# Feature-major FFN chunks from chunk 2 on, with another order of the blocks and other engines for the small additions

## The chip, the cores and the metric

The kernel runs on one core of a Trainium2 chip. The metric is the device time of one execution in microseconds (us). The kernel before takes 999.14 us, the median of three runs (998.72 to 999.98).

## The reference, cut to what matters

Two layers act on x of 256 tokens and 1024 features, in float32. Each layer is an FFN, a mixer, and a second FFN, and each of these adds its output to a scaled x and normalizes the rows:

```
def swiglu(x, w_in, w_out):                    # w_in 1024 x 5632, w_out 2816 x 1024
    gate, up = jnp.split(x @ w_in, 2, axis=-1)
    return (jax.nn.silu(gate) * up) @ w_out
x = layer_norm(ALPHA * x + 0.5 * swiglu(x, ffn1_w_in[l], ffn1_w_out[l]), ...)
x = layer_norm(ALPHA * x + mixer(x), ...)
x = layer_norm(ALPHA * x + 0.5 * swiglu(x, ffn2_w_in[l], ffn2_w_out[l]), ...)
```

The change touches the four FFNs alone. The mixers (differential attention with pooling in the first layer, a gated linear recurrence in the second) stay as they are.

## The kernel before, in words

The phases run in the order F0, AB, F1, F2, C, F3; the F's are FFNs, AB and C the mixers. The program writes out by hand, for each engine, the order of its instructions; engines wait for each other through semaphores, and nothing is planned at run time.

Every float32 matrix is split into a rounded part (hi) and a residual (lo), and a product is taken as hi x hi + hi x lo + lo x hi. Weights come in units of 128 x 2048 numbers (1 MB, two DMAs of 512 KB) into a ring of three raw buffers. ScalarE (ACT) casts a unit to hi (`split_hi`), VectorE (DVE) subtracts to get lo (`split_lo`), and only then may SyncE's queue load the unit three further on into the same raw buffer.

An FFN goes through 11 chunks of 256 hidden features. Chunk c has two units of w_in (numbers s0+3c-1 and s0+3c from chunk 1 on) and one of w_out. Chunks 0, 1, 2 and 10 are token-major: tokens are the stationary operand, the hidden values come out by tokens, and TensorE transposes them. Chunks 3 to 9 are feature-major: weights are the stationary operand, a block of 128 hidden features by (256 tokens hi, 256 tokens lo) is made by 8 matmuls of 512 columns (L2022) and 8 of 256 columns (L2029) in one PSUM bank, G[0]. ACT copies the block out (`up_copy`, L570), its two halves are added, the gate goes through silu, and VectorE multiplies (`up_product`, L1077). The order of the four blocks is gate 0, value 0, gate 1, value 1. The halves of the first three blocks are added by an accumulating DMA from GpSimd's queue (`add_halves`, L1759), those of the fourth by VectorE (`last_up_add`, L1061). Since there is one bank, a block can start only when the block before it has been copied.

Chunks 0 to 8 of the second product aren't multiplied as they stand. They use a Strassen-like scheme of seven products in seven PSUM banks, on sums and differences of hidden blocks (`hidden_sums`) and of weight blocks (`weight_sums`): 21 matmuls (L2036) for each chunk. "Early" products (banks 0, 1, 2, 4, 5) run between the blocks of the next chunk, the "late" ones (3 and 6) one chunk later. hT_hi and hT_lo hold the split hidden operand (`hid_early_hi`, L554; `hid_late_hi`, L561).

At the end of an FFN, the tail, chunk 10 is computed token-major (`project`, L1830, L1834, L1839), and the seven banks are drained: four go through ACT or VectorE into SBUF (`kept`, `SUM_PLACES`), and VectorE adds them to x_tok with four instructions of 512 columns (L1287) and one of 1024 (L1258). Then come `down` for chunks 9 and 10 and the normalization (`norm_stats`, L1114).

The parts of the code that the change touches, with the line numbers of the profile:

Of the kernel before, what the change touches and what calls it, by code (L numbers as in the profile page):

```python
# [25 lines left out]
P = 128  # L26
# [10 lines left out]
N_COPY = 3  # L37
FIRST_FM = 3
N_FM = NC - 1 - FIRST_FM
STD_CHUNK = {0: 0, 1: 1, 2: 2, NC - 1: 3}  # L40
# [35 lines left out]
def build(nc, x, positions, ln_gain, ln_bias, ffn1_w_in, ffn1_w_out, ffn2_w_in, ffn2_w_out, ab_w_in, ab_w_o,  # L76
          diff_lambda, diff_subln, pool_w, pool_scale, c_w_in, c_w_o, c_norm, hgrn_gamma, consts, out):
    with ExitStack() as ctx:
# [68 lines left out]
        halves_added = [sem(f"halves_added{b}") for b in range(4)]  # L147
# [140 lines left out]
        def tile_half(a, t):  # L288
# [59 lines left out]
        first_halves = ffn_tok[:].rearrange("p a t f -> p (a t f)").rearrange("p (b f) -> p b f", b=2)  # L348
        HALVES = {name: [first_halves[:, 0], first_halves[:, 1], region(5376 if name == BEFORE_AB else 6656, 512),
                         region(8192 if name == BEFORE_AB else 7168, 512)] for name in FFN}  # L350
# [123 lines left out]
        def _(act):  # L474
# [88 lines left out]
            def up_copy(name, c, b):  # L563

                f = SILUS[name]
                act.wait_ge(up_done, 4 * (N_FM * f + c - FIRST_FM) + b + 1)
                if c > FIRST_FM:
                    act.wait_ge(hid_product, 2 * (N_FM * f + c - FIRST_FM - 1) + b // 2 + 1)
                dst = HALVES[name][b]
                nc.scalar.copy(dst, G[0]).then_inc(up_copied, 1)  # L570

            def up_silu(name, c, j):

                act.wait_ge(halves_added[2 * j], 16 * (N_FM * SILUS[name] + c - FIRST_FM + 1))
                gate = HALVES[name][2 * j][:, 0:SEQ]
                nc.scalar.activation(gate, gate, ACT.Silu).then_inc(gate_silu, 1)  # L576

            def ffn(name, m):
# [40 lines left out]
                n = s0 + 3 * 2 + 1  # L619
                hid_early_hi(name, 1)  # L620
                hid_late_hi(name, 1)
                if m:
                    split_hi(n + 1)
                ffn_silu(name, 0, 2, G[0])
                if m == 0:
                    split_hi(n + 1)
                split_sums_hi(name, n)
                split_hi(n + 2)
                ffn_silu(name, 1, 2, G[0])
                split_plain_hi(n + 3)  # L630
                hidT_copy(name, 2, G[0])
                last = NC - 2
                for c in range(FIRST_FM, NC - 1):
                    n = s0 + 3 * c + 1
                    split_hi(n + 1)
                    if c == FIRST_FM:
                        hid_early_hi(name, c - 1)
                    up_copy(name, c, 0)
                    split_hi(n + 2)
                    if c > FIRST_FM:  # L640
                        hid_early_hi(name, c - 1)
# [3 lines left out]
                    up_silu(name, c, 0)  # L645
# [8 lines left out]
                    up_silu(name, c, 1)  # L654
# [3 lines left out]
                nc.scalar.activation(SUM_PLACES[name][:, 0], PROD[4], ACT.Copy, scale=NORMS[name][1]  # L658
                                     ).then_inc(copied_out, 1)
                act.wait_ge(hid_product, 2 * N_FM * (f + 1))  # L660
# [314 lines left out]
        def _(dve):  # L975
# [22 lines left out]
            def weight_sums(name, n, part):  # L998
# [3 lines left out]
                t1, t2, t3, t4 = (SUM_PLACES[name][:, a] for a in range(4))  # L1002
                if part == 0:
# [3 lines left out]
                    nc.vector.tensor_tensor(t1, b12, b11, ALU.subtract).then_inc(w_step1, 1)  # L1007
                    nc.vector.tensor_tensor(t3, b22, b12, ALU.subtract)
                else:
                    dve.wait_ge(w_step1, nth[n])  # L1010
                    nc.vector.tensor_tensor(t2, b22, t1, ALU.subtract).then_inc(w_step2, 1)
# [16 lines left out]
            def hidden_sums(name, c):  # L1028
# [4 lines left out]
                if c < FIRST_FM:  # L1033
                    dve.wait_ge(hidT_copied, N_COPY * f + c + 1)
                else:
                    dve.wait_ge(hid_product, 2 * (N_FM * f + c - FIRST_FM + 1))
# [19 lines left out]
            def last_up_add(name, c):  # L1056

                f = SILUS[name]
                both = HALVES[name][3]
                dve.wait_ge(up_copied, 4 * (N_FM * f + c - FIRST_FM + 1))  # L1060
                nc.vector.tensor_tensor(both[:, 0:SEQ], both[:, 0:SEQ], both[:, SEQ:], ALU.add  # L1061
                                        ).then_inc(halves_added[3], 1)

            def up_product(name, c, j):
# [1515 lines left out]
```

## Time and profile before

| | |
|---|---|
| profiled execution | 1003.51 us |
| its span, first to last instruction | 1001.8 us |
| TensorE matmul busy | 963.8 us (96%) |
| VectorE busy | 862.0 us (86%) |
| ScalarE busy | 615.4 us (61%) |
| GpSimd busy | 109.8 us (11%) |
| mean granted TensorE clock | 0.995 |
| bytes moved | 195.72 MB, 195 GB/s |

The span is one execution, taken by the profiler. "Busy" for TensorE counts the pipelined matmuls with modelled ends, so single matmuls overlap: 8 of them in a row are shown as one stretch. "Idle before" is the time in which an engine had nothing to do, with what ended it. PE is TensorE, PEld its weight loads, DVE is VectorE, ACT ScalarE, POOL GpSimd, and SPq SyncE's DMA queue. A row of a stretch has its length, then busy time and count of PE, PEld, DVE, ACT and POOL, then the granted TensorE clock (1.00 is 2.4 GHz), the share in which the DMA engines were busy, and GB/s.

### The profile page before, as it was taken

Reading aid. Unit: us, or ns where it says so; the run is one execution under the profiler, and the core shown is the slowest. Engines: PE = TensorE matmul, PEld = TensorE weight load, DVE = VectorE, ACT = ScalarE, POOL = GpSimd, SP = SyncE. Lnnn points to the kernel's source line nnn. Section 1 sums busy time; section 2 is a strip of 40 time slices with the busy share of each in tenths; the row PEclk is TensorE's granted clock in tenths of the full one; section 3 lists DMA queues with packets and bytes.
Section 4 is the critical chain, followed back from the end, with each engine's and each line's share of the span. In section 5 each row is a group of like instructions: output and inputs, shape, how many; then the busy total and the mean of one; then the engine's idle time right before and its main releaser. Section 6 shows DMA issues by size and latency. Waiting matters only on the chain.

```text
span 1001.8 us, 13771 instructions
## 1 busy us (share of the span) xinstructions
PE 963.8 (96%) x4856; PEld 803.7 (80%) x4856; DVE 862.0 (86%) x1272; ACT 615.4 (61%) x747; POOL 109.8 (11%) x148
## 2 busy tenths in 40 slices
PE   9999999999999999999999999999999999999996
PEld 7788788788887887877877887788888888887874
DVE  6998887995889889879889999899898988988785
ACT  6676666436556657565565757549898546757560
POOL 0112111000210111110001111000101100111110
PEclk9999999999999999999999999999999999999998
DMA  8779686653756786855577686646233665776831
GB/s 296 228 226 323 176 242 187 206 177 119 242 210 208 205 238 179 246 173 179 174 217 227 186 241 183 204 149 208 86 127 106 231 208 183 224 230 170 254 102 42
DMA packets 141424, 195.72 MB, mean 195 GB/s; under 512 B 7312, under 2 KB 116896, under 8 KB 141232
## 3 DMA queue, kind: packets, MB, share of 16 engines
q1 hardware_dynamic: 126032, 173.56, 52.7%
q0 software_dynamic: 14768, 20.79, 10.1%
q8 instruction: 39, 0.64, 0.3%
q10 hardware_dynamic: 560, 0.52, 0.2%
q14 instruction: 25, 0.20, 0.1%
HBM read 182.78 MB, written 1.05 MB: 184 GB/s over the span
## 4 chain that ended last, share of the span: by engine, by line
PE 53%; DMA 17%; DVE 16%; issue 6%; ACT 6%; SPq 0%; POOL 0%; ACTq 0%; DVEq 0%
DMA arena<-arena 12%; PE psum L2022 10%; PE psum L1830 9%; PE psum L1839 9%; PE psum L1834 9%; DVE w_lo L989 6%; PE psum L2029 5%; PE psum L2036 5%; DMA raw<-in_ffn_w_in 4%; ACT w_hi L499 2%; DMA ffn_tok<-ffn_tok 2%; ACT ffn_tok L570 1%; ACT arena L570 1%; DVE w_lo L1025 1%; PE psum L2467 1%
## 5 line engine op out<-in xcount | busy, mean ns | idle before, releaser
L989 DVE TENSOR_TENSOR w_lo<-raw,w_hi 128x2048 fp32r<-128x2048 f32 x125 | 284.9, 2285 | 7.8 <-ACT w_hi L499 7.3
L499 ACT CAST w_hi<-raw 128x2048 fp32r<-128x2048 f32 x125 | 237.9, 1912 | 44.8 <-DMA raw<-in_ffn_w_in 23.0
L2022 PE MATMUL psum<-xT,w_hi 128*128 128x512 f32 x896 | 225.7, 394 | 14.6 <-ACT ffn_tok L570 14.2
L2022 PEld LDWEIGHTS psum<-xT,w_hi 128*128 128x128 f32 x896 | 166.8, 189 | 60.2 <-ACT ffn_tok L570 23.9
L1830 PE MATMUL psum<-w_hi,xT 128*128 128x512 f32 x511 | 146.3, 399 | 2.9 <-DVE ffn_tok L1155 2.3
L1839 PE MATMUL psum<-w_hi,xT 128*128 128x512 f32 x511 | 142.0, 390 | 0.2 <-DVE xT L1097 0.2
L1834 PE MATMUL psum<-w_lo,xT 128*128 128x512 f32 x511 | 141.9, 390 | 0.0
L2029 PEld LDWEIGHTS psum<-xT,w_lo 128*128 128x128 f32 x896 | 122.2, 190 | 8.8
L2029 PE MATMUL psum<-xT,w_lo 128*128 128x256 f32 x896 | 124.9, 283 | 0.0
L1839 PEld LDWEIGHTS psum<-w_hi,xT 128*128 128x128 f32 x511 | 96.0, 188 | 20.8 <-DVE xT L1097 0.5
L1834 PEld LDWEIGHTS psum<-w_lo,xT 128*128 128x128 f32 x511 | 96.0, 188 | 20.2
L1830 PEld LDWEIGHTS psum<-w_hi,xT 128*128 128x128 f32 x511 | 92.6, 188 | 22.6 <-DVE ffn_tok L1155 4.3
L1759 POOL DMA_DIRECT2D ffn_tok<-ffn_tok x56 | 47.7, 851 | 429.7 <-ACT ffn_tok L570 429.7
L1025 DVE TENSOR_TENSOR w_lo<-arena,w_hi 128x2048 fp32r<-128x2048 f32 x35 | 80.0, 2285 | 0.0
L570 ACT COPY arena<-psum 128x512 f32<-128x512 f32 x56 | 32.9, 587 | 69.9 <-PE psum L2029 69.9
L2036 PE MATMUL psum<-w_lo,hT_hi 128*128 128x512 f32 x224 | 72.9, 398 | 2.1 <-DVE w_lo L1025 2.1
L2036 PE MATMUL psum<-w_hi,hT_hi 128*128 128x512 f32 x224 | 73.1, 396 | 0.6 <-ACT hT_hi L554 0.6
L511 ACT CAST w_hi<-arena 128x2048 fp32r<-128x2048 f32 x36 | 69.0, 1917 | 5.0 <-DVE arena L1013 5.0
L2036 PE MATMUL psum<-w_hi,hT_lo 128*128 128x512 f32 x224 | 67.7, 395 | 0.0
L995 DVE TENSOR_TENSOR w_lo<-raw,w_hi 128x1536 fp32r<-128x1536 f32 x36 | 63.1, 1752 | 3.5 <-ACT w_hi L505 3.5
L505 ACT CAST w_hi<-raw 128x1536 fp32r<-128x1536 f32 x36 | 53.4, 1485 | 10.8 <-PE psum L2036 8.5
L576 ACT ACTIVATE arena<-arena 128x256 f32<-128x256 f32 x28 | 11.7, 419 | 62.6 <-DMA arena<-arena 62.6
(223 smaller groups left out, 1240.8 us busy)
## 6 DMA issues: line engine op xcount, KB each, us to landing
raw<-in_ffn_w_in SPq DMA_DIRECT2D x170, 512.0 KB, 5.5
raw<-in_ffn_w_out SPq DMA_DIRECT2D x88, 512.0 KB, 4.4
raw<-in_c_w_in SPq DMA_DIRECT2D x32, 512.0 KB, 4.5
raw<-in_ab_w_in SPq DMA_DIRECT2D x16, 512.0 KB, 4.6
ffn_tok<-ffn_tok POOLq DMA_DIRECT2D x56, 128.0 KB, 5.2
raw<-in_ab_w_o SPq DMA_DIRECT2D x8, 512.0 KB, 4.1
raw<-in_c_w_o SPq DMA_DIRECT2D x8, 512.0 KB, 4.2
arena<-arena POOLq DMA_DIRECT2D x28, 128.0 KB, 6.1
```

Of the source, the lines that this page charges most:

```text
L499: nc.scalar.copy(w_hi[:, slot_of[n]], raw[:, n % RAW]).then_inc(hi_ready, 1)
L505: nc.scalar.copy(w_hi[:, PLAIN, 0:1536], raw[:, n % RAW, 512:]).then_inc(plain_hi, 1)
L511: nc.scalar.copy(w_hi[:, SUMS], SUM_PLACES[name].rearrange("p a f -> p (a f)")).then_inc(sums_hi, 1)
L989: nc.vector.tensor_tensor(w_lo[:, slot_of[n]], raw[:, n % RAW], w_hi[:, slot_of[n]].bitcast(F32), ALU.subtract).then_inc(lo_ready, 1)
L995: nc.vector.tensor_tensor(w_lo[:, PLAIN, 0:1536], raw[:, n % RAW, 512:], w_hi[:, PLAIN, 0:1536].bitcast(F32), ALU.subtract).then_inc(plain ...
L1025: nc.vector.tensor_tensor(w_lo[:, SUMS], SUM_PLACES[name].rearrange("p a f -> p (a f)"), w_hi[:, SUMS].bitcast(F32), ALU.subtract).then_in ...
L1830: nc.tensor.matmul(dst, a_hi, b_hi, start=first, stop=False)
L1834: ins = nc.tensor.matmul(dst, a_hi, b_lo, start=False, stop=final and last)
L1839: ins = nc.tensor.matmul(dst, a_lo, b_hi, start=False, stop=final and last)
L2022: nc.tensor.matmul(G[0], w_hi[:, slot_of[n + kh], at:at + P], xT_both[:, 4 * kh + k].rearrange("p a s -> p (a s)"), start=kh == k == 0, st ...
L2029: ins = nc.tensor.matmul(G[0][:, 0:SEQ], w_lo[:, slot_of[n + kh], at:at + P], xT_hi[:, 4 * kh + k], start=False, stop=kh == 1 and k == 3)
L2036: return nc.tensor.matmul(PROD[p], a[:, A_OF[p] * P:(A_OF[p] + 1) * P], w[:, slot, part * 512:(part + 1) * 512], start=False, stop=stop)
```

## The change

Chunk 2 becomes feature-major, so there are eight feature-major chunks in an FFN instead of seven. The blocks come in the order gate 0, gate 1, value 0, value 1. The halves of the two gates are added by the accumulating DMA; the two values are added by one VectorE instruction of 512 columns. One silu serves both gates, and one multiplication all of the chunk. ACT's order in a chunk changes, and VectorE's too. The late products of hidden chunk 0 move behind block 0 of chunk 2. The first two weight differences are one instruction (with the sign of t1 turned, and with it the sign of bank 4's scale). What VectorE added to x_tok is added by five accumulating DMAs of GpSimd's queue, and the statistics of the normalization wait for them. In F1 the tables for mixer C are copied before the first hidden sums instead of in chunk 2.

The core of the diff:

```
-N_COPY = 3
-FIRST_FM = 3
+N_COPY = 2
+FIRST_FM = 2
 ...
                 nc.scalar.copy(dst, G[0]) ...
+                nc.scalar.copy((UPS[name] if b // 2 else GATES)[:, b % 2], G[0]).then_inc(up_copied, 1)
+            def gates_silu(name, c):
+                for j in range(2):
+                    act.wait_ge(gate_added[j], 16 * (N_FM * SILUS[name] + c - FIRST_FM + 1))
+                nc.scalar.activation(GATES[:, :, 0:SEQ], GATES[:, :, 0:SEQ], ACT.Silu).then_inc(gate_silu, 1)
 ...
 ACT, in ffn:
                 split_plain_hi(s0 + 7)
-                hid_early_hi(name, 1)
-                hid_late_hi(name, 1)
-                (casts, ffn_silu and hidT_copy of token-major chunk 2)
                 for c in range(FIRST_FM, NC - 1):
                     n = s0 + 3 * c + 1
                     split_hi(n + 1)
-                    if c == FIRST_FM:
-                        hid_early_hi(name, c - 1)
+                    hid_early_hi(name, c - 1)
                     up_copy(name, c, 0)
                     split_hi(n + 2)
-                    if c > FIRST_FM:
-                        hid_early_hi(name, c - 1)
                     hid_late_hi(name, c - 1)
                     up_copy(name, c, 1)
                     split_sums_hi(name, n)
-                    up_silu(name, c, 0)
                     up_copy(name, c, 2)
 ...
                     up_copy(name, c, 3)
-                    up_silu(name, c, 1)
+                    gates_silu(name, c)
 ...
 VectorE, in weight_sums:
-                    nc.vector.tensor_tensor(t1, b12, b11, ALU.subtract).then_inc(w_step1, 1)
-                    nc.vector.tensor_tensor(t3, b22, b12, ALU.subtract)
+                    nc.vector.tensor_tensor(SUM_PLACES[name][:, 0:3:2], w[:, 1:3], b12.unsqueeze(1).to_broadcast([P, 2, 512]),
+                                            ALU.subtract).then_inc(w_step1, 1)
 VectorE, in norm_stats:
+                if name in FFN:
+                    for i in ((2, 4), (0, 1, 3))[t]:
+                        dve.wait_ge(x_added[i], 16 * (SILUS[name] + 1))
 VectorE, in ffn:
                 for c in range(FIRST_FM, NC - 1):
                     n = s0 + 3 * c + 1
+                    if c > FIRST_FM:
+                        up_add(name, c - 1)
+                        up_product(name, c - 1)
+                        hidden_sums(name, c - 1)
+                    weight_sums(name, n, 0)
+                    weight_sums(name, n, 1)
+                    hid_early_lo(name, c - 1)
+                    split_lo(n + 1)
+                    hid_late_lo(name, c - 1)
                     beside(name, c)
                     split_lo(n + 2)
                     split_sums_lo(name, n)
-                    up_product(name, c, 0)
+                    if c < last:
                         split_plain_lo(n + 3)
+                split_lo(n + 3)
+                up_add(name, last)
+                up_product(name, last)
-                (five add_to_x on VectorE)
 ...
 GpSimd:
+            def add_gates(name, chunks):
+                for c in chunks:
+                    for j in range(2):
+                        pool.wait_ge(up_copied, 4 * (N_FM * SILUS[name] + c - FIRST_FM) + j + 1)
+                        pool.dma_start(GATES[:, j, 0:SEQ], GATES[:, j, SEQ:], accum_op=ALU.add).then_inc(gate_added[j], 16)
+            def add_sums(name):
+                pool.wait_ge(copied_out, 2 * f + 1)
+                add_to_x(0, 1, high, kept[0])
+                pool.wait_ge(copied_out, 2 * f + 2)
+                add_to_x(1, 1, low, SUM_PLACES[name][:, 0])
+                add_to_x(2, 0, low, SUM_PLACES[name][:, 0])
+                pool.wait_ge(moved_out, 2 * f + 1)
+                pool.wait_ge(x_added[1], 16 * (f + 1))
+                add_to_x(3, 1, low, kept[1])
+                pool.wait_ge(moved_out, 2 * f + 2)
+                pool.wait_ge(x_added[2], 16 * (f + 1))
+                pool.dma_start(x_tok[:, 0] (both halves), kept_both (twice), accum_op=ALU.add).then_inc(x_added[4], 16)
 ...
 TensorE:
-                j, g = divmod(b, 2)
+                g, j = divmod(b, 2)
+            def feature_chunk(name, s0, c):
+                up_block(name, n, c, 0)
+                late_products(name, p - 3, c - 2, c == FIRST_FM)
+                up_block(name, n, c, 1)
+                high(0, 1, 2) ... weight_rest(0, 1)
+                up_block(name, n, c, 2)
+                weight_rest(2) ... token_rest(last, 0, 1, 2) ... high(4)
+                up_block(name, n, c, 3)
+                high(5) ... weight_rest(4, 5) ... token_rest(last, 4, 5)
```

## Rows read from the trace of the kernel before

**Rows 1.** The page: shares of the chain that ended last, by engine.
```profile
PE 53%; DMA 17%; DVE 16%; issue 6%; ACT 6%; SPq 0%; POOL 0%; ACTq 0%; DVEq 0%
```
**Rows 2.** Stretches: middles of F0 to F3, then tails of F0 to F2.
```profile
34.14:170.05 135.91, 131.88 (x675) 110.31 (x674) 118.35 (x153) 87.81 (x96) 20.21 (x25) 1.00 0.79 237
306.02:443.47 137.45, 131.19 (x676) 110.28 (x674) 119.14 (x149) 86.30 (x94) 17.83 (x21) 1.00 0.74 219
496.07:633.95 137.88, 133.06 (x675) 111.53 (x674) 124.59 (x147) 86.48 (x94) 17.86 (x21) 0.99 0.74 219
833.82:969.40 135.58, 131.14 (x676) 110.26 (x674) 114.34 (x138) 87.25 (x96) 17.84 (x21) 1.00 0.72 215
...
170.05:194.40 24.35, 22.42 (x103) 17.77 (x102) 22.57 (x27) 10.44 (x12) 1.14 (x1) 1.00 0.51 172
443.47:467.50 24.03, 22.62 (x102) 17.59 (x101) 22.51 (x27) 10.44 (x12) 0.56 (x1) 1.00 0.52 176
633.95:659.00 25.05, 22.22 (x101) 17.57 (x100) 22.41 (x27) 10.29 (x11) 0.56 (x1) 1.00 0.50 168
```
**Rows 3.** Groups of instructions: full matmuls of the blocks (busy, mean ns | idle before).
```profile
L2022 PE MATMUL psum<-xT,w_hi 128*128 128x512 f32 x896 | 225.7, 394 | 14.6 <-ACT ffn_tok L570 14.2
```
**Rows 4.** In order of time, F0 around chunk 9's block 0 (start, us, what).
```profile
152.21 1.98 PE L2022 MATMUL psum<-xT,w_hi 128*128 128x512 f32 x8
...
154.02 0.42 ACT L576 ACTIVATE arena<-arena 128x256 f32<-128x256 f32 x1 [2.19 <-DMA arena<-arena]
...
154.97 0.63 PE L2036 MATMUL psum<-w_hi,hT_hi 128*128 128x512 f32 x2
...
156.77 2.12 PE L2022 MATMUL psum<-xT,w_hi 128*128 128x512 f32 x8 [0.25 <-ACT ffn_tok L570]
```
**Rows 5.** In order of time, VectorE in F2, product to product.
```profile
575.55 1.75 DVE L1469 RECIPROCAL arena<-arena 128x256 f32<-128x256 f32 x1
...
581.75 0.42 DVE L1077 TENSOR_TENSOR arena<-ffn_tok 128x256 f32<-128x256 f32 x1
...
591.29 0.87 DVE L1475 TENSOR_TENSOR arena<-arena 128x688 f32<-128x688 f32 x1
...
597.69 0.43 DVE L1077 TENSOR_TENSOR arena<-ffn_tok 128x256 f32<-128x256 f32 x1 [1.01 <-DMA ffn_tok<-ffn_tok]
```
**Rows 6.** In order of time, ScalarE near chunk 2 of F0, F1, F2, F3.
```profile
34.40 0.60 ACT L546 COPY arena<-psum 128x512 f32<-128x512 f32 x1
...
41.42 1.90 ACT L499 CAST w_hi<-raw 128x2048 fp32r<-128x2048 f32 x1
...
308.62 0.73 ACT L554 CAST hT_hi<-arena 128x640 fp32r<-128x640 f32 x1 [2.17 <-DVE arena L1042]
...
310.99 1.92 ACT L499 CAST w_hi<-raw 128x2048 fp32r<-128x2048 f32 x1 [1.33 <-DMA raw<-in_ffn_w_in]
...
502.16 1.92 ACT L499 CAST w_hi<-raw 128x2048 fp32r<-128x2048 f32 x1 [2.45 <-DMA raw<-in_ffn_w_in]
...
839.16 1.92 ACT L499 CAST w_hi<-raw 128x2048 fp32r<-128x2048 f32 x1 [1.71 <-DMA raw<-in_ffn_w_in]
```
**Rows 7.** Stretches in F2: TensorE idle, then the stretch after it.
```profile
529.07:530.94 1.87, 0.01 (x2) 0.01 (x1) 1.87 (x2) 0.58 (x1) 0.00 (x0) 1.00 0.81 174
530.94:534.48 3.54, 3.54 (x9) 2.77 (x10) 3.54 (x6) 2.20 (x2) 0.00 (x0) 0.52 0.79 254
```
**Rows 8.** By line: landing of L1759's 128 KB adds, then L1745's 512 KB loads.
```profile
DMA to landing us min/median/max: 2.7/5.8/7.4
...
DMA to landing us min/median/max: 3.8/6.9/11.1
```
**Rows 9.** In order of time, the tail of F0.
```profile
171.04 0.58 ACT L658 ACTIVATE arena<-psum 128x512 f32<-128x512 f32 x1
...
185.97 0.69 DVE L1114 SCALAR_TENSOR_TENSOR x_tok<-psum,x_tok 128x512 f32<-128x512 f32 x1
...
190.09 0.42 DVE L1155 TENSOR_TENSOR ffn_tok<-psum,ffn_tok 128x256 f32<-128x256 f32 x1
```

More of the change, by code:

```diff
@@ L567, in up_copy @@
                 if c > FIRST_FM:
[L568 to L576, printed above, removed]
+                    act.wait_ge(hid_product, N_FM * f + c - FIRST_FM)
+                nc.scalar.copy((UPS[name] if b // 2 else GATES)[:, b % 2], G[0]).then_inc(up_copied, 1)
[3 more added lines that the diff above has]
+                nc.scalar.activation(GATES[:, :, 0:SEQ], GATES[:, :, 0:SEQ], ACT.Silu).then_inc(gate_silu, 1)
             def ffn(name, m):
@@ L1001, in weight_sums @@
                 b12, b11, b22, b21 = (w[:, a] for a in range(4))
-                t1, t2, t3, t4 = (SUM_PLACES[name][:, a] for a in range(4))
+                t1, t2, _, t4 = (SUM_PLACES[name][:, a] for a in range(4))
                 if part == 0:
@@ L1251, in ffn @@
                 split_lo(n)
-                dve.wait_ge(moved_out, 2 * f + 2)
-                dve.wait_ge(dve_step, first)
-                add_to_x(1, slice(0, 512), kept[1])
-                ffn_hidden(name, 0, G[0], 6, ffn_tok[:, 1, 0])
-                dve.wait_ge(dve_step, second)
-                x0 = x_tok[:, 0].rearrange("p (h f) -> p h f", h=2)
-                step(nc.vector.tensor_tensor(x0, x0, kept_both.unsqueeze(1).to_broadcast([P, 2, 512]), ALU.add))
+                ffn_hidden(name, 0, G[0], 4, ffn_tok[:, 1, 0])
                 split_lo(n + 1)
@@ L2116, in feature_chunk @@
                 high(4)
-                if first:
-                    high(5)
                 up_block(name, n, c, 3)
-                if not first:
-                    high(5)
+                high(5)
                 pe.wait_ge(sums_lo, nth[p])
@@ L2124, in feature_chunk, with late_products @@
                 token_rest(last, 4, 5).then_inc(pairs_done if last else early_used, 1)
-                if first:
-                    pe.wait_ge(late_hi, late)
-                    high(3)
-            def late_products(name, p, c, last=False):
+            def late_products(name, p, c, first=False, last=False):
                 f = SILUS[name]
@@ L2133, in late_products @@
                 pe.wait_ge(sums_hi, nth[p])
-                high(3, 6)
+                high(3, 6, start=first)
                 pe.wait_ge(sums_lo, nth[p])
```

210 lines of the change are left out of this document (51 added, 159 removed).

## The prediction

> **What bounds the kernel now.** I began with the chain that ended last. TensorE holds 53% of it, and one accumulating DMA, arena<-arena, 12%, more than any single line of an engine [rows 1]. Then the busy time by stage. I cut each FFN into a middle and a tail. The middle runs from the point at which the products of hidden chunk 0 on banks 3 and 6 start (call it S) to the first matmul of the last chunk's projection (call it E). The four middles take 135.91, 137.45, 137.88 and 135.58 us with TensorE busy 131 to 133 of them; the first three tails idle 1.93, 1.41 and 2.83 us [rows 2]. So TensorE is the bound, and only its holes and the number of its instructions can move the time.
>
> The groups say where the holes are: 14.2 us before L2022, released by the ACT copies of blocks [rows 3]. One chunk in order of time shows why. ACT's silu at 154.02 has waited 2.19 us for the DMA add of block 2; only then come the weight cast and the copy of block 0, and TensorE starts block 1 at 156.77 after 0.25 us idle [rows 4]. Without the wait the chunk is: a block 152.21 to 154.97, 2.76 us; six products from 154.97, which would end 0.41 us before 156.77 (0.25 idle and some 0.16 of restart), 1.39 us, or 0.232 each. Four blocks and 21 products make 11.08 + 4.87 = 15.95 us. The chunks take 16.5 to 17.
>
> **The middle after the change.** Chunk 2 turns feature-major, so the middle holds eight such chunks and six late products: 8 x 15.95 + 1.39 = 129.0 us if nothing stalls. That is 6.9, 8.4, 8.9 and 6.6 us under the four middles of today. (In it: token-major chunk 2 has 48 full matmuls and four transposes against 32 full and 32 half ones, about even; its wait for the hidden product goes; the block-1 holes go.)
>
> Would the holes go? In the new ACT order nothing waits for the gate DMAs before block 3 is copied. The gates' add for j=1 is issued about 8 us after the start of block 0 and is needed at 15.6; it lands within 7.4 us at the worst [rows 8]. So this wait is covered. Now the copy of block 0 stands behind the early hidden cast, which stands behind add, product and four hidden sums on VectorE. Add and product follow the copy of block 3 and are 0.69 us each at 512 columns (as the instruction of that width in [rows 9]), the sums about 1.0: done some 2.1 us into the new block 0; the cast (0.73) and copy (0.6, both [rows 6]) end at 3.6, and block 1 wants it at 4.16. Margin 0.5 us. VectorE's own work in a chunk was 15.94 - 1.01 = 14.93 with 0.87 of extra work in it, so 14.0 [rows 5]. Two products and an add at 256 columns (0.34 apart, 1.1 in all) become two instructions at 512 (1.4), the fused weight sum saves between nothing and 0.2, taken as 0: 14.3 of 15.95. Only in FFN F2 is it more, for four chunks: a reciprocal of 1.75 and its add, 2.2 us [rows 5], gives 16.5. With 1 us of slack to use up first, that costs 1.2 us. Bounds for this step: 0 if slack takes it, 0.7 a chunk (the old hole stays) if the margin is wrong.
>
> **The new hole in chunk 2.** ACT's list from chunk 2 on is: cast of unit s0+8, early hidden cast, copy of block 0. Formerly that weight cast came after the hidden casts and nothing on TensorE hung on it for long. Now TensorE's block 1 waits for the copy behind it. The unit needs its raw buffer, which is freed by the residual of unit s0+5, and lands late: ACT's cast started at 310.99 in F1, at 502.16 in F2 and at 839.16 in F3, each with an idle wait for that DMA before it, and at 41.42 in F0 [rows 6]. Nothing in the change makes it land earlier. From there 1.92 (cast), 0.73 (hidden cast), 0.6 (copy) and the handovers, 0.2: block 1 starts 3.45 us after the cast. TensorE is ready for it at S + 2.76 + 1.39. S is 306.02, 496.07 and 833.82 [rows 2]; so it idles 4.3, 5.4 and 4.6 us. In F0 S is 34.14 and the hidden copy that block 0 waits for ends at 35.0, so block 0 starts about 1.0 late and idles another 5.6 in two pieces: block 1 at 44.9 against 38.3, 6.6 lost. Together 20.9 us. If the DMA lands as early as the shortest of such chains allows, 1.5 us less each.
>
> The clock answers to such holes. When TensorE idled 1.87 us at 529.07, the granted clock stood at 0.52 for the next 3.54 us, then at 1.00 again [rows 7]: that is the lower level, 1.2 GHz, and 0.48 x 3.54 = 1.7 us lost. The tail of F2, with 2.83 us in three holes, stayed at 1.00 [rows 2]. The new ones are longer than 1.87 in all four FFNs: 4 x 1.7 = 6.8 us. Bounds 0 and 10.
>
> Middles: F0 129.0 + 6.6 + 1.7 = 137.3 (1.4 slower); F1 129.0 + 4.3 + 1.7 = 135.0 (2.4 faster); F2 129.0 + 5.4 + 1.7 + 1.2 = 137.3 (0.6 faster); F3 129.0 + 4.6 + 1.7 = 135.3 (0.3 faster). Sum 1.9 us faster, out of the 30.8 that a middle without holes would give.
>
> **The tails.** VectorE loses its five adds to x. Its lateness makes the three holes of each tail (two before transposes, one before the last products): the idle of [rows 2] and some 0.16 for each restart make 2.4, 1.9 and 3.3 us, and none in F3. Against this, the statistics of token tile 0 now wait for two DMAs in a row, 256 KB and then 512 KB, and behind them on VectorE stands the last hidden product, for which TensorE waits. ACT's copy at 171.04, 1.0 us after E, no longer waits for the DMA add and can end at about E - 0.5. Then the second add is issued at E + 0.5, the last one when it has landed. A 128 KB add lands after 2.7 to 7.4 us, median 5.8; the 512 KB loads of the same queue after 3.8 to 11.1, median 6.9 [rows 8]. No row shows an add of 256 or 512 KB; the sum of both lies between 6.5 and 18.5 us. I take 6.7 + 7.5, near the medians and a little above them for the size: landed at E + 14.8. VectorE needs 4.5 us from the first statistics (185.97) to the end of the product at 190.51 [rows 9], and TensorE, with the earlier holes gone, wants it at E + 18.1, so the adds have to land by E + 13.6. What comes later is a hole: 1.2 us, and 1.6 with restart and jitter, short of what lowered the clock. Tails: 7.6 - 3 x 1.6 = 2.8 us faster; in F3, where no weight loads compete, the adds land well before y is done and nothing changes. If the adds are quick, 7.6; at the other end holes of 5.5 us with a clock loss of 1.7, 14 us slower.
>
> The Trainium skill (DMA: Bandwidth & Descriptors, Anatomy of one DMA, SWDGE path) gives about 2.0 us plus the bytes at 436 GB/s for one DMA, an estimate of 2.6 and 3.2 us for these two, and no hole in the tail. The trace speaks against it beside weight loads: its 128 KB adds take 5.8 us where that gives 2.3. By the page the tails would be 7.6 us faster.
>
> Edits at nothing: the C tables moved forward in F1 lie where VectorE waits for ACT's hidden copy, and cost at most one instruction of 1.2 us if it did not; the products on banks 3 and 6 of chunk 0 only move; the dropped semaphores cost nothing.
>
> **Sum.** 1.9 + 2.8 = 4.7 us. The profiled execution took 1003.5 us (span 1001.8 and 1.7 around it), so 998.8 for its like; the median of the runs is 4.4 lower, and I forecast 994.4 us.
>
> **Rivals.** (a) The holes are cheaper: the clock stays at 1.00 through chunk 2 (6.8 us) or the adds to x land in time (4.8 us), or both: 983 to 989 us. For it: F3's unloaded tail. Against: [rows 7]. Chance 0.24. (b) The adds to x come late and become the tail's bound, in F0, F1 and F2. It decides from a landing at E + 17 on: then the holes are 3.5 us and more and lower the clock too, 5 us each, and at E + 19 7 us: 1004 to 1012 us, slower. For it: two dependent DMAs beside weight loads. Against: the weight loads themselves come earlier, as VectorE frees buffers earlier. Chance 0.13. (c) The margin of 0.5 us in the full chunks isn't there: with 0.35 us of hole left in each of 32 chunks, 11 us, 1005 us. For it: ACT copies block 0 behind a chain through VectorE that ends 2.1 us into the block. Against: VectorE has 1.6 us to spare. Chance 0.10. (d) The parts cancel, 997.1 to 1001.1 us: the change gives back in chunk 2 what it takes from the other chunks, 0.13 with the forecast's upper edge. The forecast, 990 to 997 us: 0.40.
>
> Differences under 0.2% (2 us) are about what a measurement of this kernel can't tell from none. Faster: 0.40 + 0.24 = 0.64; within 0.2%: 0.13; slower: 0.13 + 0.10 = 0.23. The range of 8 in 10 runs from 984 to 1006 us; the forecast's own is 990 to 997.
>
> **What would show it.** Right: arena<-arena gone from the chain of waits; no idle before block 1 in chunks 3 to 9 and a period near 15.95 us; in chunk 2 of each FFN one idle of 4 to 6 us before block 1, ended by the ACT copy, ACT before it waiting for raw<-in_ffn_w_in, and the clock at half after it. In the tails the statistics waiting for x_tok DMAs, 1 to 2 us. Wrong: chunk 2 without that hole, chunks of 16.3 us or more, or a wait for x_tok above 4 us.

## The result and the profile after

The changed kernel takes 1023.0 us (median of 4 runs, 1021.0 to 1027.1) against 999.6: the ratio is 1.024, 95% interval 1.0207 to 1.0273. I had forecast 994.4 us, range 984 to 1006. The time is 28.6 us over the forecast. Its profiled execution took 1023.0 us with a span of 1020.4, so unlike that of before (1003.5, above its median) it stands at its own median. In the two traces the change costs 18.6 us of span. Of the other 4.9 us between the medians, 4.0 lie in the choice of the execution, since before's was at the slow end of its runs (996.2 to 1003.6 us in 21 runs taken later), and 0.9 outside the span (2.6 us in after's execution, 1.7 in before's).

The page of after, shares of the chain that ended last, by engine and then the start of the list by line [rows 1]:

```profile
PE 72%; DVE 13%; DMA 9%; issue 3%; ACT 2%; POOL 0%; SPq 0%; DVEq 0%; ACTq 0%; POOLq 0%
PE psum L1981 19%; PE psum L1995 12%; PE psum L1988 10%; PE psum L1790 9%; PE psum L1794 9%; PE psum L1799 9%; DMA x_tok<-arena 5%; DVE w_lo L972 4%; DMA raw<-in_ffn_w_in 4%; PE psum L2371 1%; PE psum L1783 1%; DVE w_lo L1008 1%; PE psum L2357 1%; DVE stats L1098 1%; DVE arena L1410 1%
```

arena<-arena is gone from it, as forecast. In its place stand the adds to x with 5%; the weight loads of w_in hold 4%, as they did before.

The same stretches as in [rows 2], middles of F0 to F3 and tails of F0 to F2. Columns: busy us (instructions) of PE, PEld, DVE, ACT, POOL, then granted clock, DMA share, GB/s. The first four run from S to E; the next three are the first part of the tails, and end at the same instruction as those of before. S is now the point from which block 0 of chunk 2 could start:

```profile
34.10:175.03 140.93, 132.67 (x688) 113.51 (x687) 123.04 (x138) 89.98 (x93) 17.09 (x22) 0.98 0.74 226
316.33:451.89 135.56, 131.68 (x687) 113.34 (x686) 121.92 (x133) 88.20 (x91) 14.70 (x18) 0.97 0.73 219
511.23:649.16 137.93, 133.45 (x688) 112.84 (x686) 128.33 (x132) 88.03 (x91) 14.71 (x18) 0.98 0.72 215
851.67:987.54 135.87, 131.94 (x687) 113.49 (x686) 117.80 (x121) 88.22 (x91) 14.76 (x18) 0.97 0.72 211
...
175.03:204.64 29.61, 24.56 (x104) 19.81 (x102) 19.13 (x22) 9.73 (x10) 4.61 (x5) 0.88 0.69 189
451.89:482.72 30.83, 23.19 (x103) 18.89 (x102) 19.09 (x23) 9.74 (x10) 4.07 (x5) 0.89 0.68 180
649.16:677.14 27.98, 23.31 (x103) 18.97 (x102) 19.16 (x23) 9.74 (x10) 4.06 (x5) 0.94 0.73 199
```

The middles change by +5.0, -1.9, 0.0 and +0.3 us, 3.5 in sum (forecast: 1.9 faster). From E to the next S it is +5.3, +6.7 and +2.6 us, and +0.5 behind the last E: 15.2 (forecast: 2.8 faster).

**The full chunks** do what was forecast. In order of time, ScalarE and TensorE in F0, chunk 7: ScalarE's copy of block 0 ends at 129.42, block 1 starts at 130.02 with no idle before it, block 2 at 133.95, and block 1 of the next chunk at 145.95. That is 15.93 us a chunk (forecast 15.95) where the old one had an idle before block 1 [rows 4]. The copy is 0.60 us ahead of the block that needs its bank; the forecast's margin was 0.5:

```profile
128.83 0.59 ACT L570 COPY ffn_tok<-psum 128x512 f32<-128x512 f32 x1
...
130.02 1.98 PE L1981 MATMUL psum<-xT,w_hi 128*128 128x512 f32 x8
133.48 0.63 PE L1995 MATMUL psum<-w_lo,hT_hi 128*128 128x512 f32 x2
133.95 1.98 PE L1981 MATMUL psum<-xT,w_hi 128*128 128x512 f32 x8
145.95 1.98 PE L1981 MATMUL psum<-xT,w_hi 128*128 128x512 f32 x8
```

**The hole in chunk 2** is there as forecast. F1 in order of time (here ScalarE's lines, then TensorE's): the weight cast waits 4.70 us for its raw DMA, the hidden cast and the copy of block 0 follow, and TensorE starts block 1 after 3.88 us of idle. Then the window from block 1's start to block 2's, which holds 3.92 us of work at full clock (2.76 and five products of 0.232) and takes 6.62 at a granted clock of 0.57:

```profile
321.47 1.90 ACT L500 CAST w_hi<-raw 128x2048 fp32r<-128x2048 f32 x1 [4.70 <-DMA raw<-in_ffn_w_in]
323.27 0.72 ACT L555 CAST hT_hi<-arena 128x640 fp32r<-128x640 f32 x1
323.90 0.58 ACT L570 COPY ffn_tok<-psum 128x512 f32<-128x512 f32 x1
...
324.53 3.78 PE L1981 MATMUL psum<-xT,w_hi 128*128 128x512 f32 x8 [3.88 <-ACT ffn_tok L570]
331.15 1.98 PE L1981 MATMUL psum<-xT,w_hi 128*128 128x512 f32 x8
...
324.53:331.15 6.62, 6.62 (x22) 5.59 (x22) 5.15 (x4) 3.31 (x4) 1.09 (x2) 0.57 0.91 274
```

129.0 us for a middle without holes (the forecast's figure), 3.88 of hole and 2.70 of clock make 135.6; measured 135.56. F3 adds up as well: 129.0 + 3.93 + 2.93 against 135.87. The group that stands for [rows 3] shows that the time spent waiting for ScalarE's copies is not less, only moved from many small waits to few long ones: 18.9 us instead of 14.2:

```profile
L1981 PE MATMUL psum<-xT,w_hi 128*128 128x512 f32 x1024 | 261.0, 398 | 19.7 <-ACT ffn_tok L570 18.9
```

F0 has one that I had not forecast, before block 2 of chunk 4, behind a weight cast that waited 4.77 us:

```profile
83.27 1.90 ACT L500 CAST w_hi<-raw 128x2048 fp32r<-128x2048 f32 x1 [4.77 <-DMA raw<-in_ffn_w_in]
...
86.01 2.11 PE L1981 MATMUL psum<-xT,w_hi 128*128 128x512 f32 x8 [2.81 <-ACT ffn_tok L570]
```

**The tail** is where the sum breaks. F0 in order of time (GpSimd's issues, VectorE's statistics, TensorE), then the landings of the 256 KB adds (L1701) and the 512 KB adds (L1716):

```profile
174.76 1.72 POOL L1701 DMA_DIRECT2D x_tok<-arena  x2 [3.31 <-ACT arena L641]
182.65 0.84 POOL L1701 DMA_DIRECT2D x_tok<-arena  x1 [6.18 <-DMA x_tok<-arena]
184.00 1.19 POOL L1716 DMA_DIRECT2D x_tok<-arena  x1 [0.50 <-DMA x_tok<-arena]
...
193.58 0.69 DVE L1096 SCALAR_TENSOR_TENSOR x_tok<-psum,x_tok 128x512 f32<-128x512 f32 x1 [5.58 <-DMA x_tok<-arena]
...
198.18 0.69 PE L1965 MATMUL psum<-ident,ffn_tok 128*128 128x128 f32 x2 [5.05 <-DVE ffn_tok L1137]
198.52 1.20 PE L1790 MATMUL psum<-w_hi,hT_hi 128*128 128x512 f32 x2
...
DMA to landing us min/median/max: 3.2/6.3/8.3
...
DMA to landing us min/median/max: 5.0/9.5/11.9
```

E is 175.03 and the last add of tile 0 lands at 193.50, E + 18.5; in F1 and F2 it lands at E + 21.0 and E + 18.1. TensorE idles 5.05, 7.64 and 4.67 us before its last hidden transposes, and two matmuls in a row then take 1.20 and 1.05 us instead of 0.71 and 0.62. The landings above are over all four FFNs. In F0, F1 and F2 alone, beside the weight loads, the 256 KB adds took 5.6 to 8.3 us and the 512 KB adds 9.5 to 11.9. In F3, where no weight load was under way, they took 3.2 to 4.3 and 5.0 us, and were in time.

### The profile page after: what moved, and what is told of

Its sections match the earlier page's. It is cut to its first block, busy times and chain, and to the rows that moved or that the text cites. A ratio compares the mean times of both kernels' runs of the same rounds, so it can differ in the third digit from the quotient of the medians.

```text
span 1020.4 us, 13819 instructions
## 1 busy us (share of the span) xinstructions
PE 969.8 (95%) x4904; PEld 818.9 (80%) x4904; DVE 861.3 (84%) x1188; ACT 619.4 (61%) x727; POOL 111.1 (11%) x148
## 3 DMA queue, kind: packets, MB, share of 16 engines
q0 software_dynamic: 15280, 24.46, 11.6%
HBM read 182.78 MB, written 1.05 MB: 180 GB/s over the span
## 4 chain that ended last, share of the span: by engine, by line
PE 72%; DVE 13%; DMA 9%; issue 3%; ACT 2%; POOL 0%; SPq 0%; DVEq 0%; ACTq 0%; POOLq 0%
PE psum L1981 19%; PE psum L1995 12%; PE psum L1988 10%; PE psum L1790 9%; PE psum L1794 9%; PE psum L1799 9%; DMA x_tok<-arena 5%; DVE w_lo L972 4%; DMA raw<-in_ffn_w_in 4%; PE psum L2371 1%; PE psum L1783 1%; DVE w_lo L1008 1%; PE psum L2357 1%; DVE stats L1098 1%; DVE arena L1410 1%
## 5 line engine op out<-in xcount | busy, mean ns | idle before, releaser
L972 DVE TENSOR_TENSOR w_lo<-raw,w_hi 128x2048 fp32r<-128x2048 f32 x125 | 285.1, 2285 | 14.8 <-ACT w_hi L500 14.4
L1981 PE MATMUL psum<-xT,w_hi 128*128 128x512 f32 x1024 | 261.0, 398 | 19.7 <-ACT ffn_tok L570 18.9
L1981 PEld LDWEIGHTS psum<-xT,w_hi 128*128 128x128 f32 x1024 | 195.7, 192 | 65.8 <-ACT ffn_tok L570 22.8
L1988 PEld LDWEIGHTS psum<-xT,w_lo 128*128 128x128 f32 x1024 | 143.1, 195 | 11.1 <-DVE w_lo L972 0.7
L1988 PE MATMUL psum<-xT,w_lo 128*128 128x256 f32 x1024 | 146.1, 286 | 0.5 <-DVE w_lo L972 0.5
L1790 PE MATMUL psum<-w_hi,xT 128*128 128x512 f32 x447 | 128.6, 398 | 0.5 <-DVE arena L1519 0.4
L1799 PE MATMUL psum<-w_hi,xT 128*128 128x512 f32 x447 | 124.7, 390 | 0.2 <-DVE xT L1076 0.2
L1794 PE MATMUL psum<-w_lo,xT 128*128 128x512 f32 x447 | 124.7, 390 | 0.0
L1698 POOL DMA_DIRECT2D ffn_tok<-ffn_tok x64 | 54.4, 850 | 520.8 <-ACT ffn_tok L570 520.8
L1799 PEld LDWEIGHTS psum<-w_hi,xT 128*128 128x128 f32 x447 | 83.9, 188 | 18.3 <-DVE xT L1076 0.5
L1794 PEld LDWEIGHTS psum<-w_lo,xT 128*128 128x128 f32 x447 | 83.9, 188 | 17.7
L1790 PEld LDWEIGHTS psum<-w_hi,xT 128*128 128x128 f32 x447 | 80.8, 188 | 16.2 <-issue 0.8
L570 ACT COPY ffn_tok<-psum 128x512 f32<-128x512 f32 x64 | 37.5, 586 | 49.1 <-PE psum L1988 49.1
```

Source lines behind the costliest of these rows:

```text
L570: nc.scalar.copy((UPS[name] if b // 2 else GATES)[:, b % 2], G[0]).then_inc(up_copied, 1)
L972: nc.vector.tensor_tensor(w_lo[:, slot_of[n]], raw[:, n % RAW], w_hi[:, slot_of[n]].bitcast(F32), ALU.subtract).then_inc(lo_ready, 1)
L1790: nc.tensor.matmul(dst, a_hi, b_hi, start=first, stop=False)
L1794: ins = nc.tensor.matmul(dst, a_hi, b_lo, start=False, stop=final and last)
L1799: ins = nc.tensor.matmul(dst, a_lo, b_hi, start=False, stop=final and last)
L1981: nc.tensor.matmul(G[0], w_hi[:, slot_of[n + kh], at:at + P], xT_both[:, 4 * kh + k].rearrange("p a s -> p (a s)"), start=kh == k == 0, st ...
```

## The experiments

All times are medians, with the ratio to the kernel before and its 95% interval. The kernel before was run again beside each group of experiments (999.3, 999.7 and 999.8 us); the changed kernel was not, and stands at its 1023.0.

### Adds to x back on VectorE

```
-                if name in FFN:
-                    for i in ((2, 4), (0, 1, 3))[t]:
-                        dve.wait_ge(x_added[i], 16 * (SILUS[name] + 1))
+                first = add_to_x(1, slice(0, 512), SUM_PLACES[name][:, 0])
+                second = add_to_x(0, slice(0, 512), SUM_PLACES[name][:, 0])
...
-                    add_sums(name)
```

> The changed kernel with one part undone: the five adds to x of each FFN are VectorE instructions again and the statistics wait for no DMA. Theory (the tail is longer because the second DMA add of tile 0 lands at E + 18 to 21 and the last hidden product stands behind the statistics on VectorE): the holes of 5.05, 7.64 and 4.67 us before the last transposes go, with the lower clock after them, and the small stalls of the tail of before come back. The stretches from E to the next S return to before's, 5.3 + 6.7 + 2.6 us shorter: 1008.4 us. Rival (the new order of VectorE's tail, sums_out and casts, makes the holes, not the landing): holes of 3 us or more stay at the same place, 1016 us or more.

Measured: 1000.25 us, ratio 1.0009 (0.9993 to 1.0024). The holes before the last transposes are gone, so the theory stands on their cause; but the gain is 22.8 us, not 14.6. The tail of F0 in order of time shows why. These are the three instructions before which TensorE stalled in the kernel before, now without idle. So not even the old stalls come back, although all five adds are VectorE's again:

```profile
184.88 0.38 PE L1978 MATMUL psum<-ident,ffn_tok 128*128 128x128 f32 x2
187.41 0.62 PE L1812 MATMUL psum<-w_hi,hT_lo 128*128 128x512 f32 x2
193.31 0.38 PE L1978 MATMUL psum<-ident,ffn_tok 128*128 128x128 f32 x2
```

From E to the next S this kernel takes 2.8, 2.4 and 3.5 us less than the one before, 8.7 in all: these are the stalls that my prediction booked (7.6) to the adds' move. They went with the rest of the change. The kernel with token-major chunk 2, further below, keeps little but the new order of the blocks and of the engines' lists, and from E to chunk 3 of the next FFN it is shorter than before by 2.5, 3.0 and 3.6 us: so the new order did it. The adds by DMA cost 23.4 us in the traces (8.1 + 9.1 + 6.2).

### ScalarE's copies ahead of the late cast in chunk 2; both mends

```
+                    if c == FIRST_FM:
+                        up_copy(name, c, 0)
+                        hid_early_hi(name, c - 1)
+                        split_hi(n + 1)
+                        up_copy(name, c, 1)
+                        split_hi(n + 2)
+                        hid_late_hi(name, c - 1)
```

> The changed kernel with ScalarE's list of chunk 2 alone in another order: copy of block 0, early hidden cast, cast of unit s0+8, copy of block 1, cast of unit s0+9, late hidden cast. Theory (TensorE waits for the copy behind the cast whose raw DMA lands late, and the half clock follows the hole): the holes of 4.25, 3.88, 4.00 and 3.93 us go and the stretches at half clock after them (2.8, 2.7, 2.5, 2.9 us lost) with them; 27 us less, 996 us, middles of F1 and F3 near 129.5. Rival 1 (the half clock comes at that place for another reason): holes gone, clock still at half there, 16.7 us less, 1006 us. Rival 2 (the late DMA only moves the hole to block 2, behind the next cast): a hole of 2 to 3.5 us before block 2, 1012 us or more.

> Both of the foregoing edits at once. Theory: the two costs are independent and add, 14.6 + 27 us: 981.5 us, 1.8% under the kernel before; what is left of the change is then nine steady chunks without a hole in each FFN. Rival (the gain of the steady chunks is given back elsewhere once the holes go, as ScalarE or the weight loads become late): 990 us or more.

Measured: 1004.7 us (1.0042, 1.0023 to 1.0061) alone and 981.0 us (0.981, 0.979 to 0.983) with the adds back. The order gains 18.3 us without the other mend and 19.2 with it, the adds 22.8 and 23.7: the costs are independent, and together 42.0 us, as expected to half a microsecond, though each part was off by some 8. The long holes of chunk 2 and the half clock behind them go in F1 to F3. What the order did not reach is a shorter hole later in chunk 2, where TensorE waits for the cast of the weight sums, which stands behind both late weight casts. F0 and F1 with the copies first, adds still by DMA:

```profile
49.80 0.67 PE L2003 MATMUL psum<-w_hi,hT_hi 128*128 128x512 f32 x1 [1.90 <-ACT w_hi L512]
...
329.71 0.51 PE L2003 MATMUL psum<-w_hi,hT_hi 128*128 128x512 f32 x1 [1.08 <-ACT w_hi L512]
```

So rival 2 was right in kind, and its hole small. F1's middle is 130.5 us.

### Tile 0's adds first in the queue

```
+                add_to_x(2, 0, low, SUM_PLACES[name][:, 0])
                 add_to_x(1, 1, low, SUM_PLACES[name][:, 0])
-                add_to_x(2, 0, low, SUM_PLACES[name][:, 0])
...
                                ).then_inc(x_added[4], 16)
+                pool.wait_ge(x_added[1], 16 * (f + 1))
+                add_to_x(3, 1, low, kept[1])
```

> The changed kernel, adds to x still by DMA, but in another order on GpSimd's queue: tile 0's 256 KB add before tile 1's, and tile 0's 512 KB add before tile 1's last one. Theory Q (each add waits in the queue for the one issued before it): tile 0's adds land 3 to 5 us earlier, the tail holes shrink from 5.05, 7.64 and 4.67 to 1 to 4 us, 1011 to 1015 us. Rival D (the adds share no order, each takes its time beside the weight loads): the landing moves by under 1.5 us, holes of 4 us and more stay, 1019 to 1023 us.

Measured: 1011.4 us (1.0123, 1.0092 to 1.0154), 11.6 us less than the change. Tile 0's last add lands at E + 15.9, 15.9 and 14.9. The landings of the 512 KB add, and TensorE's holes:

```profile
DMA to landing us min/median/max: 5.1/7.8/9.7
...
195.98 0.44 PE L1964 MATMUL psum<-ident,ffn_tok 128*128 128x128 f32 x2 [2.47 <-DVE ffn_tok L1137]
466.54 0.44 PE L1964 MATMUL psum<-ident,ffn_tok 128*128 128x128 f32 x2 [2.48 <-DVE ffn_tok L1137]
658.88 0.44 PE L1964 MATMUL psum<-ident,ffn_tok 128*128 128x128 f32 x2 [1.55 <-DVE ffn_tok L1137]
```

Theory Q: an add that stands ahead in the queue delays the one behind it, by 2.6, 5.2 and 3.1 us over both. Single executions differ here, but not by enough to undo this: with the old order of the adds they landed at E + 17.9 to E + 20.4 in the kernel with the copies first, and at E + 19.9 to E + 21.1 in the next one below. A good part of the lateness is left, though. In this kernel too the 512 KB add takes 7.6 to 9.7 us in F0, F1 and F2 and 5.1 in F3, where no weights load; so the holes do not shrink to the 1 us end of the range.

### The last hidden product ahead of the statistics

```
-                norm_stats(name, 0)
-                norm_gain(name, 0, (0,))
                 ffn_hidden(name, 1, G[1], 5, ffn_tok[:, 1, 1])
-                norm_gain(name, 0, (1,))
                 last_hidT(name, 1)
+                norm_stats(name, 0)
+                norm_gain(name, 0, (0,))
+                norm_gain(name, 0, (1,))
```

> The changed kernel, adds to x still by DMA, but in VectorE's tail the last hidden product and the cast residual of its transposed form stand before the statistics of tile 0 instead of behind them. Theory L (the landing of the adds is the bound): TensorE's last transposes of the hidden product no longer wait, but the next stage's transposes of x wait for the statistics instead; the holes of 5.05, 7.64 and 4.67 us move to there and shrink by about 1 us each; 1018 to 1021 us. Rival V (only the place of the product in VectorE's list makes the hole, x is not wanted early): the holes go with their clock loss, 23 us less, as with the adds on VectorE: about 1000 us.

Measured: 1023.45 us (1.023, 1.0199 to 1.026), no gain. The hole moves to the next stage's transposes of x:

```profile
201.79 1.97 PE L1783 MATMUL psum<-ident,x_tok 128*128 128x128 f32 x8 [4.63 <-DVE x_tok L1126]
```

4.63, 5.82 and 5.24 us there: the landing is the bound, VectorE's order is not. The three holes sum to 15.7 us instead of 17.4, less than the 3 us of shrinking expected. The edit also has a cost of its own: behind the last E, where no add was late, its trace takes 37.0 us instead of 32.8. So the equal time may hide a small gain, but nothing near the rival's 23 us.

### F0's tables spread over the chunks

```
                 add_gates("F0", (2, 3))
                 pool.dma_start(poolw, ...
+                add_gates("F0", (4,))
                 pool.dma_start(band, ...
-            load_gb(0)
+            add_gates("F0", (5,))
+            load_gb(0, (0,))
+            add_gates("F0", (6,))
+            load_gb(0, (1,))
```

> The kernel with both mends (adds to x on VectorE, ScalarE's copies first in chunk 2), and in F0 the five loads of tables and gains that GpSimd issues in a row after the gate adds of chunk 3 spread over chunks 3 to 6, one a chunk. Theory (these loads, 1 MB of gains among them, make the weight load late on which the hole of 2.6 to 3.2 us before block 1 of chunk 5 rests): that hole and the half clock after it go, the middle of F0 shrinks from 135.7 to some 131.5, 977 us. Rival (the weight load is late there whatever GpSimd loads): a hole of 2 us or more stays, 980 us or more.

Measured: 976.8 us (0.9774, 0.9751 to 0.9797). F0's middle, counted here from its first block, goes from 135.7 to 132.3 us, and no idle is left at that place (the expectation names it wrongly: it is block 2 of chunk 4). So these loads on GpSimd's queue did it. With both mends alone TensorE had waited there:

```profile
80.01 3.48 PE L2002 MATMUL psum<-xT,w_hi 128*128 128x512 f32 x8 [2.61 <-ACT ffn_tok L570]
```

### The weight sums ahead of unit s0+9 in chunk 2

```
                         up_copy(name, c, 1)
+                        split_sums_hi(name, n)
                         split_hi(n + 2)
...
+                    if c == FIRST_FM:
+                        split_sums_lo(name, n)
+                        split_lo(n + 2)
```

> The kernel with both mends, and in chunk 2 the cast of the weight sums before the cast of unit s0+9 on ScalarE, its residual before that unit's on VectorE. Theory: the holes of 0.87, 1.45, 1.04 and 0.45 us before the product on bank 4 in chunk 2 go: 3 to 4 us less, 977.5 us. Rival (the residual of unit s0+9 then frees its raw buffer later and the next weight load is late): new waits for raw<-in_ffn_w_in in chunk 3, no gain or a loss, 981 us or more.

Measured: 985.1 us (0.9854, 0.9823 to 0.9884), 4 us slower than without it: the rival's time, and in part its mechanism. The holes before the product on bank 4 are gone, but block 1 of chunk 3 has a new one in all of F0 to F3, here F1. There ScalarE waits 0.15 us for its raw DMA and then 2.21 for VectorE's hidden sums, which come late behind the residuals; so in F1 this hole is VectorE's, and not the late load that the rival names. In F0 the hole of 2.61 us in chunk 4 grows to 5.47, and there it is the load: the weight cast ahead of it waits 6.56 us for its raw DMA, 4.56 with both mends alone:

```profile
329.06 0.72 ACT L555 CAST hT_hi<-arena 128x640 fp32r<-128x640 f32 x1 [2.21 <-DVE arena L1034]
330.32 2.12 PE L2007 MATMUL psum<-xT,w_hi 128*128 128x512 f32 x8 [1.39 <-ACT ffn_tok L570]
```

### Token-major chunk 2 kept; then F0's tables spread too

```
+                products(name, s0 + 4, None, 0, (3, 6), sums_used, True)
+                token_chunk(name, s0, 2)
                 for c in range(FIRST_FM, NC - 1):
                     feature_chunk(name, s0, c)
```

> The changed kernel with chunk 2 token-major as before (products of hidden chunk 0 on banks 3 and 6 ahead of it, the C tables in its place) and the adds to x on VectorE: the order of blocks gate, gate, value, value with its adds is all that is left of the change, on chunks 3 to 9. Theory (the gain is the full chunks' period of 15.94 us, the token-major chunk 2 costs what the feature-major one does without its hole): middles near 131, with F0 some 3 us more, no hole in the tails, 978 to 983 us, the same as with both mends within 3 us. Rival (feature-major chunk 2 carries part of the gain): middles 134 or more, 988 us or more.

> The kernel with token-major chunk 2 and adds to x on VectorE, and F0's loads of tables and gains spread over chunks 4 to 7. Theory: the hole of 1.50 us before block 1 of chunk 6 in F0 goes with its restart, 1.5 to 2 us less, 973.5 us, the fastest of all. Rival: nothing is gained, since the weight load is late there for its own reasons, 975 us.

Measured: 975.1 us (0.9761, 0.9738 to 0.9784) and 974.0 us (0.9735, 0.9714 to 0.9756), the latter 25.8 us under the kernel before and the fastest with the next one. The order gate, gate, value, value carries the whole gain, with what belongs to it: one silu, the two VectorE instructions of 512 columns, the new lists of ScalarE and VectorE, and the fused weight difference. These were not taken apart. With F0's tables spread in both, turning chunk 2 as well costs 2.8 us even with ScalarE's list mended (976.8 against 974.0). The spreading gains 1.1 us here, less than expected. In the last kernel one group shows that waiting for ScalarE is nearly over, 2.0 us where [rows 3] has 14.6:

```profile
L2030 PE MATMUL psum<-xT,w_hi 128*128 128x512 f32 x896 | 222.4, 390 | 2.0 <-ACT arena L547 2.0
```

### Tile 1's adds by DMA in the fastest kernel; the adds alone in the kernel before

```
-                first = add_to_x(1, slice(0, 512), SUM_PLACES[name][:, 0])
+                if name in FFN and t == 1:
+                    for i in (0, 1, 3):
+                        dve.wait_ge(x_added[i], 16 * (SILUS[name] + 1))
```

> The same kernel, with the three adds to tile 1 of x as DMAs again, in which the statistics of tile 1 have some 10 us more to wait, and the two to tile 0 on VectorE. Theory (VectorE has room in the tail, so that taking its adds away buys nothing; the DMAs are harmless where there is slack): the same time within 1 us, 973.5 us. Rival 1 (VectorE's adds cost TensorE something in the tail): 2 us or more less. Rival 2 (the DMAs are late for tile 1 too, or delay the weight loads of the next stage): holes of 1 us or more after the tail, 977 us or more.

Measured: 973.9 us (0.9735, 0.971 to 0.9759), the same time. Where they have slack the DMAs do no harm, and these three adds on VectorE cost TensorE nothing.

The last run put all five adds of before on DMA and changed nothing else.

> The kernel before, with one part of the change alone: the five adds to x of each FFN by DMA. My prediction held that VectorE's adds make the small holes of the old tail (0.47, 0.99 and 0.47 us of idle in F0), which then would go here. Theory now (they come from VectorE starting its tail late, behind the halved products of the last chunk, since they are gone with the adds still on VectorE once the blocks are reordered): at least two of the three stay at 0.3 us or more, and the late landing adds its hole before the last transposes, 3 to 6 us in F0, F1 and F2 with the lower clock after it; 1012 to 1020 us. Rival (the adds made them): the two earlier stalls are gone, 1003 to 1010 us.

Measured: 1017.2 us (1.0171, 1.0134 to 1.0208). The adds by DMA cost 17.4 us here, at the medians. The two traces hold 11.3 of it, 10.9 of that between the E's and chunk 3 of the FFN after; the rest lies again in the choice of the executions. The last add of tile 0 lands at E + 17.8, 18.9 and 18.3. TensorE in the tail of F0, then ScalarE:

```profile
185.52 0.73 PE L1843 MATMUL psum<-w_hi,hT_hi 128*128 128x512 f32 x2 [1.73 <-ACT hT_hi L671]
194.99 0.69 PE L2019 MATMUL psum<-ident,ffn_tok 128*128 128x128 f32 x2 [2.37 <-DVE ffn_tok L1159]
...
183.29 1.90 ACT L500 CAST w_hi<-raw 128x2048 fp32r<-128x2048 f32 x1 [4.77 <-DMA raw<-in_ab_w_in]
```

The time is the theory's, but the theory of the old stalls does not hold as it was put. The first stall (0.47 us) is gone with the adds, as the rival has it, and the last has the landing's hole in its place. The one between them is there and longer (1.73 us instead of 0.99), but it is not the old one. In the kernel before, TensorE waited there for VectorE (hT_lo, L1301); here it waits for ScalarE's cast behind a weight cast that waited 4.77 us for its raw DMA, 2.70 before. That load landed 7.1 us after its issue instead of 4.6, with adds to x under way beside it. In F1 and F2 the same cast waits 4.56 and 4.64 us (3.47 and 2.68 before), and the stalls are 1.76 and 1.87. So the adds by DMA do harm in a second way, by making a weight load late. Either of two things removes the first stall, the adds' leaving or the blocks' new order. That the old second one goes is shown only with the new order.

## Why the prediction was wrong

By its own steps, with the forecast first and then what was measured in the profiled executions:

- **The middle without holes**, 129.0 us of 8 x 15.95 + 1.39: right. Full chunks take 15.93, the margin of 0.5 us held, and F1 and F3 add up to 0.1 us. (Four blocks of 2.76 us are 11.04 and not the 11.08 of the sum; the slip is 0.04 us a chunk, and the measured period lies between the two.)
- **"Only in FFN F2 is it more"**, 1.2 us: right in kind. Four of F2's chunks take 16.57, 16.67, 16.65 and 16.28 us, 2.4 over the period; the slack of 1 us that I let it use up first was not there.
- **The hole in chunk 2**, 6.6 + 4.3 + 5.4 + 4.6 = 20.9 us: right in place and cause, a little too large. Idle before block 1 is 4.25, 3.88, 4.00 and 3.93, with 1.2 us more in F0 before it; some 17.3. From the start of the weight cast to block 1 it took 3.06 us in all four, where I had summed 3.45, and in F2 the load came 0.8 us earlier after S than before.
- **"0.48 x 3.54 = 1.7 us lost"** to the clock after each: too small. The stretches from block 1 to block 2 take 6.73, 6.62, 6.42 and 6.85 instead of 3.92: 2.8, 2.7, 2.5 and 2.9, 10.9 us against 6.8. [rows 7] had a hole of half the length. But the same hole does not always cost this: with the adds back on VectorE the stretches take 6.86, 5.62, 5.59 and 5.62, so 1.7 us lost in three of four, the forecast's own figure.
- **Edits at nothing**: the loads of tables and gains in F0 were not weighed. Before, the weight cast behind them waited 1.10 us (at 89.41); after, 4.77, and TensorE 2.8 behind it. That the loads do it is shown by spreading them; why the wait grew is not.
- **The tails: "Its lateness makes the three holes of each tail", VectorE's adds removed, 7.6 us faster.** The size was nearly right (8.7), the credit mostly wrong: once the blocks are reordered, the stalls are gone with the adds still on VectorE.
- **"I take 6.7 + 7.5 ... landed at E + 14.8"**: the step that failed. The landings were E + 18.5, 21.0 and 18.1. GpSimd issues tile 0's 256 KB add right behind tile 1's, and it takes some 8 us; the 512 KB add is issued behind tile 1's last one and takes 9.5, 11.9 and 9.5. I priced two DMAs in a row and left the two of tile 1 out. Issued ahead of these, they took 6.0 to 7.6 and 7.6 to 9.7 us; my 14.2 in all is 1 to 2 us short even of that (16.2, 16.1 and 15.2 from the first issue to the last landing).
- **"The adds have to land by E + 13.6"**: right. 18.5, 21.0 and 18.1 give holes of 4.9, 7.4 and 4.5 where 5.05, 7.64 and 4.67 were measured; with tile 0 first, 15.9, 15.9 and 14.9 give 2.3, 2.3 and 1.3 against 2.47, 2.48 and 1.55.
- **"short of what lowered the clock"**: wrong with the size. The last stretch up to the transposes of x takes 5.6, 4.3 and 4.4 us instead of 3.0: 5.2 us lost.

The sum of the errors in the traces: tails 17.5 us (the adds cost 23.4 against 4.8, less 1.1 of larger gain on the old stalls), middles 5.4 (clock 4.1, F0's unforeseen hole 2.8, F2 1.2, less 3.6 of chunk-2 holes; the rest is F0's restarts), the end 0.5: 23.4. To this come the 4.4 us that I took off because before's profiled execution stood above its median, while after's stands at its own, and the 0.9 us more outside its span: 28.7 in all, with rounding.

Rival (b) named this course, with its point of decision (E + 17) and its price at E + 19 (7 us each), and had a chance of 0.13; its 1004 to 1012 us were too low, as it kept everything else of the forecast. The bounds were wrong as well as the value: 18.5 us was meant as the worst for two landings, which would be E + 19.0, and F1's came at E + 21.0. The two adds ahead of them cost 2.6 to 5.2 us; with these added, most of the range lies beyond E + 13.6, and the rival ought to have been the forecast.

The Trainium skill (DMA: Bandwidth & Descriptors, Anatomy of one DMA, SWDGE path) gives an estimate of 2.6 and 3.2 us for these adds. In F3, where no weights load, the trace has 3.2 to 4.3 and 5.0 us; beside weight loads it has medians of 7.1 and 9.5, so neither agrees. The Trainium skill (DMA: Bandwidth & Descriptors, Two DMAs through the same engine are not ordered) says that descriptors within a queue of one engine start in order but are pipelined; the 2.6 to 5.2 us that tile 0 gains by going first agree with it.

## What to carry to other kernels

A DMA that relieves an engine is priced by its landing, and that by everything ahead of it in its queue and beside it on the DMA engines; put it only where its reader has several times its unloaded time (here 5.0 us became 11.9), and ask which loads it will slow down beside it. Before crediting an edit with the end of a stall, ask whether another part of the same change would end it too; here the reordering ended all the stalls by itself, and the adds by DMA brought nothing on top of it. An engine's list should place the copies that free a bank of TensorE ahead of any cast that can wait for a weight load.

## What the runs showed of the hardware

- A 256 KB accumulating DMA within SBUF landed after 3.2 to 3.3 us with no weight load under way (4.3 when issued right behind another) and after 5.6 to 8.3 beside weight loads, median 7.1; a 512 KB one after 5.0 and after 9.5 to 11.9.
- The loading goes both ways: beside the adds of the last experiment a 512 KB weight load took 7.1 us, where it took 4.6 in the kernel before.
- TensorE's granted clock fell to its lower level of 1.2 GHz (0.50 in the window 198.18 to 203.79 of after) behind every hole of over 3 us between matmuls that these traces hold. Shorter holes went either way: half clock after 1.86, 1.90, 2.37, 2.48, 2.53, 2.61 and 2.74 us, full clock after 2.47, 2.62, 2.81 and 2.89. Behind the chunk-2 holes the half clock cost 2.5 to 2.9 us each in after's execution; in the three other kernels that keep these holes it cost 1.6 to 2.9 us, and about 1.7 in eight cases of twelve. I had not expected the cost to vary so, and no run isolates what decides it.
